# First weight blocks over the first rows, and attentions that open by their own counts

## Reference

```python
def even_layer(x, norm, w_in, ...):
    h = rmsnorm_2(x, norm)
    qa, ka, va, qb, kb, vb, gate = _split(h @ w_in, SPLIT_E)      # 3328 columns
    ...                                                            # two attentions
    o = jnp.concatenate([oa, ob], -1) * jax.nn.silu(gate)
    return o @ w_out
def odd_layer(x, norm, w_in, ...):
    h = rmsnorm_2(x, norm)
    cq, ckv, kpe, qd, kd, vd, gate = _split(h @ w_in, SPLIT_O)    # 2976 columns
    ...
```

## Time and profile before

| | us |
|---|---|
| median of 3 runs | 3122.36 |
| the runs | 3122.36, 3122.58, 3114.90 |
| the profiled execution | 3115.78 |
| its span | 3114.2 |
| TensorE busy | 2986.1 (96%) |
| VectorE, ScalarE, GpSimd busy | 1611.6, 1198.7, 1084.1 |

### The profile page before, as it was taken

One profiled execution on the slowest core, in us unless ns is written; L12 is line 12 of the kernel. 1 busy time (PEld: TensorE's weight loads), 2 busy tenths in 40 slices (PEclk: granted clock), 3 DMA queues, 4 the chain that ended last, 5 costly groups with the idle time before them and its releaser, 6 DMA issues.

```text
span 3114.2 us, 50002 instructions
## 1 busy us (share of the span) xinstructions
PE 2986.1 (96%) x18212; PEld 2593.1 (83%) x18212; DVE 1611.6 (52%) x3091; ACT 1198.7 (38%) x2181; POOL 1084.1 (35%) x702
## 2 busy tenths in 40 slices
PE   7999998999999999998999999999999999999989
PEld 6688866778888888888999888987897989988877
DVE  3899738342222232313038378971113958778861
ACT  3311264342221211313124356761323646667750
POOL 2222120432222235662226334335321554432235
PEclk9999998999999999999999999999999999999999
DMA  4123331431111114442296343405236763231223
GB/s 144 61 101 116 107 76 30 136 115 48 47 47 51 50 47 129 123 141 89 84 222 214 104 120 86 118 21 174 100 123 211 214 165 81 69 80 41 83 85 129
DMA packets 224247, 325.70 MB, mean 105 GB/s; under 512 B 81414, under 2 KB 167302, under 8 KB 221910
## 3 DMA queue, kind: packets, MB, share of 16 engines
q1 hardware_dynamic: 188934, 277.29, 29.8%
q10 hardware_dynamic: 33360, 39.98, 3.7%
q0 software_dynamic: 1792, 6.29, 0.7%
HBM read 229.95 MB, written 93.57 MB: 104 GB/s over the span
## 4 chain that ended last, share of the span: by engine, by line
PE 71%; DVE 8%; issue 2%; ACT 2%; POOL 1%; DMA 1%; SPq 0%; DVEq 0%; POOLq 0%; ACTq 0%
PE psum L2261 15%; PE psum L528 13%; PE psum L2047 8%; PE psum L2464 8%; PE psum L1097 6%; PE psum L1066 6%; PE psum L1077 5%; DVE arena L2865 3%; PE psum L780 2%; PE psum L758 2%; PE psum L769 1%; DVE arena L2854 1%; PE psum L1112 1%; PE psum L3224 1%; DVE above_mixer L840 1%
## 5 line engine op out<-in xcount | busy, mean ns | idle before, releaser
L2261 PE MATMUL psum<-parts_ffn 128*128 128x512 f32 x2112 | 482.2, 391 | 3.8 <-DVE parts_ffn L2218 3.8
L2261 PEld LDWEIGHTS psum<-parts_ffn 128*128 128x128 f32 x2112 | 398.4, 189 | 87.2 <-issue 2.2
L528 PE MATMUL psum<-parts_even,parts_ffn 128*128 128x256 f32 x2496 | 305.5, 285 | 5.2 <-DVE parts_ffn L2598 4.0
L528 PEld LDWEIGHTS psum<-parts_even,parts_ffn 128*128 128x128 f32 x2496 | 303.3, 194 | 5.9 <-DVE parts_ffn L2598 4.5
L2331 DVE SCALAR_TENSOR_TENSOR arena<-psum,arena 128x1023 f32<-128x1023 f32 x88 | 112.9, 1282 | 328.2 <-ACT arena L2315 322.0
L528 PE MATMUL psum<-parts_odd 128*128 128x248 f32 x2304 | 271.8, 280 | 4.9 <-ACT arena L568 2.2
L528 PEld LDWEIGHTS psum<-parts_odd 128*128 128x128 f32 x2304 | 269.7, 191 | 6.2 <-DVE parts_odd L2218 4.5
L568 ACT ACTIVATE arena<-psum 128x256 f32<-128x256 f32 (+2 forms) x240 | 87.8, 376 | 423.7 <-PE psum L528 419.7
L444 PE MATMUL psum<-parts_mixer 128*128 128x512 f32 x912 | 210.0, 391 | 0.3 <-DVE parts_mixer L287 0.3
L444 PEld LDWEIGHTS psum<-parts_mixer 128*128 128x128 f32 x912 | 170.5, 188 | 35.7 <-DVE parts_mixer L287 0.5
L1139 ACT ACTIVATE both<-psum 128x512 fp32r<-128x512 f32 x256 | 140.1, 596 | 107.6 <-PE psum L1077 107.0
(11 more groups left out here) (344 smaller groups left out, 5913.0 us busy)
## 6 DMA issues: line engine op xcount, KB each, us to landing
arena<-ffn_up_b SPq DMA_DIRECT2D x44, 512.0 KB, 3.3
arena<-ffn_down_k SPq DMA_DIRECT2D x44, 512.0 KB, 3.6
arena<-x SPq DMA_DIRECT2D x8, 2048.0 KB, 8.6
arena<-w_in_e SPq DMA_DIRECT2D x13, 1024.0 KB, 6.7
e_tokens<-arena ACTq DMA_DIRECT2D x26, 512.0 KB, 3.2
x<-arena SPq DMA_DIRECT2D x24, 512.0 KB, 3.8
arena<-w_in_o SPq DMA_DIRECT2D x12, 992.0 KB, 6.7
o_tokens<-arena ACTq DMA_DIRECT2D x24, 496.0 KB, 3.0
```

The source lines that it names most:

```text
L528: last = pe.matmul(self.bank(t), self.hT[:, a, k, t * P:(t + 1) * P], self.weights.parts[:, self.weights.slot(s), b, k, :], start=(k, a, b ...
L2261: last = pe.matmul(self.core.psum[:, 4 * u + 2 * s + h, :], parts[:, s, a, k, :], self.hT[:, b, k, h * HALF:(h + 1) * HALF], start=(k, a, ...
```

## The change

The first two blocks of `tok3a` and `tok4a` go in the order `FRONT`: (block 0, tiles 0 to 3), (block 1, tiles 0 to 3), (block 0, tiles 4 to 7), (block 1, tiles 4 to 7). The turns of half 1 stand behind positions 4 and 6 of this order instead of 1 and 3, and the hold for all parts behind position 7. ScalarE takes the first four positions out in the stage before: position 0 after `finish` of row tile 6, position 1 ahead of the parts of half 1, positions 2 and 3 behind its fourth part. In `tok4a` these four go to a stage of their own (`front_stage`) in the weight ring. `tok1`'s opening stands ahead of `feat1` on ScalarE, behind a hold for the scores. The first two of `expd` are added by TensorE itself, and `folded` is waited for at the first `back` step.

```diff
+    FRONT = [(s, 4 * h + j) for h in range(2) for s in range(2) for j in range(TT // 2)]
-    def multiply(self, pe, i, s, t):
+    def multiply(self, pe, i, s, t, at=None):
         if t == 0:
             self.weights.wait(pe, i, s)
-        pe.wait_ge(self.act_out, 16 * i + 8 * s + t + 1)
+        pe.wait_ge(self.act_out, (16 * i + 8 * s + t if at is None else at) + 1)
...
-        for s in range(2):
-            for t in range(TT):
-                if t == 4:
-                    hold(pe, self.second_half)
-                self.multiply(pe, 0, s, t)
-                if s == 0:
-                    self.between(pe, t)
+        for at, (s, t) in enumerate(self.FRONT):
+            if at == TT:
+                hold(pe, self.second_half)
+            self.multiply(pe, 0, s, t, at)
+            self.between(pe, at)
...
-    def take_out(self, act, i, s, t):
+    def take_front(self, act, at):
+        s, t = self.FRONT[at]
+        self.take_out(act, 0, s, t, at)
+    def take_out(self, act, i, s, t, front=None):
         h, j = divmod(t, TT // 2)
+        at, before = 16 * i + 8 * s + t, 2 * i + s
+        if front is not None:
+            at, h, before = front, front // 4 % 2, front // TT
+        stage = self.stage[:, h] if self.front_stage is None or front is None or front >= 4 else self.front_stage
         if j == 0:
-            act.wait_ge(self.stored[h], 16 * (2 * i + s) + 1)
+            act.wait_ge(self.stored[h], 16 * before + 1)
...
+        if self.between is not None:
+            for at in range(4, 2 * TT):
+                self.take_front(act, at)
+        for i, s in paired(act, self.blocks, 1 if self.between is not None else 0):
...
+        pe.sem_inc(self.expd, 2)
...
-        pe.wait_ge(self.folded, 1)
...
             g = n // 2
+            if g == 0:
+                pe.wait_ge(self.folded, 1)
...
-        act.sem_inc(self.expd, 2)
...
-        for k in range(KT) if t is None else {1: range(4), 3: range(4, KT)}.get(t, ()):
+        for k in range(KT) if t is None else {4: range(4), 6: range(4, KT)}.get(t, ()):
             self.turn(pe, 1, k)
...
             act.activation(self.ys[t], self.xs[:, t], ACT.Copy, scale=spot).then_inc(self.scaled, 1)
+            if t == 6 and self.take_next is not None:
+                self.take_next(act, 0)
...
         for k in range(KT):
+            if k in (0, 4) and self.take_next is not None:
+                for at in (1,) if k == 0 else (2, 3):
+                    self.take_next(act, at)
             part(act, 1, k)
...
+        tok1_opening = Part()
         add(scores)
...
+        add(tok1_opening)
         add(feat1)
...
+        def open_tok1(act):
+            hold(act, scores.done)
+            tok1.start_scalar(act)
+        tok1.opened_before = True
+        tok1_opening.methods = (None, None, open_tok1, None, None)
...
-                        [(0, 128, 13, e_heads)], [start_e + [first.done[n // 4]] for n in range(TT)], first_bank=4, stage_slots=1)
+                        [(0, 128, 13, e_heads)], [start_e + first.stored_blocks(2) + [first.done[n // 4]] for n in range(TT)], first_bank=4, stage_slots=1)
...
+        project.front_stage = shaped(core.arena[:, ring_at:ring_at + 4 * 248], (4, 248))
```

More of the change, by code:

```diff
@@ L492, in __init__ @@
         self.between, self.second_half, self.first_apart, self.opened_before = None, [], False, False
-        self.scalar_pieces, self.gates_from = {}, blocks * width
+        self.scalar_pieces, self.gates_from, self.front_stage = {}, blocks * width, None
         self.act_out = core.sem(f"{name}_act_out")
@@ L567, in take_out @@
             if a < b:
-                last = act.activation(self.stage[:, h, j, a:b], self.bank(t)[:, a:b], function)
+                last = act.activation(stage[:, j, a:b], self.bank(t)[:, a:b], function)
         last.then_inc(self.act_out, 1)
         if j == TT // 2 - 1:
-            act.wait_ge(self.act_out, 16 * i + 8 * s + t + 1 + len(self.banks))
+            act.wait_ge(self.act_out, at + 1 + len(self.banks))
             columns = self.out[t - j:t + 1, :, bass.ds((i * 2 + s) * self.width, self.width)]
-            act.dma_start(columns.rearrange("t p c -> p t c"), self.stage[:, h]).then_inc(self.stored[h], 16)
+            act.dma_start(columns.rearrange("t p c -> p t c"), stage).then_inc(self.stored[h], 16)
     def scalar(self, act):
@@ L579, in scalar @@
         if self.scalar_pieces:
-            for u in range(self.blocks * TT):
+            for at in range(4, 2 * TT):
+                self.take_front(act, at)
+            for u in range(2 * TT, self.blocks * TT):
                 b, t = divmod(u, TT)
@@ L585, in scalar @@
             return
-        for i, s in paired(act, self.blocks):
+        if self.between is not None:
+            for at in range(4, 2 * TT):
+                self.take_front(act, at)
+        for i, s in paired(act, self.blocks, 1 if self.between is not None else 0):
             for t in range(TT):
@@ L1960, in __init__ @@
         self.xs, self.ys, self.gain, self.after, self.retire = xs, ys, gain, after, retire
-        self.open_next, self.open_by_scalar, self.before_split = None, None, {}
+        self.open_next, self.open_by_scalar, self.before_split, self.take_next = None, None, {}, None
         self.K = w.shape[1]
@@ L2514, in turn_second @@
     def turn_second(self, pe, t):
-        for k in {1: range(4), 3: range(4, KT)}.get(t, ()):
+        for k in {4: range(4), 6: range(4, KT)}.get(t, ()):
             self.turn(pe, 1, k)
@@ L2563, in finish @@
             act.activation(self.y_of(t), self.x_of(t), ACT.Copy, scale=spot).then_inc(self.scaled, 1)
+            if t == 6:
+                self.take_next(act, 0)
         def part(act, h, k):
@@ L2572, in scalar @@
         self.order(act, self.high, drain, finish, part)
-        for k in range(KT):
+        self.take_next(act, 1)
+        for k in range(4):
+            part(act, 1, k)
+        for at in (2, 3):
+            self.take_next(act, at)
+        for k in range(4, KT):
             part(act, 1, k)
@@ L3575, in build @@
         project.first_apart = project.opened_before = True
-        down.open_next = project.start_scalar
+        down.open_next, down.take_next = project.start_scalar, project.take_front
         down.next_load = project.weights.load_first
@@ L3670, in build @@
         project.first_apart = project.opened_before = True
-        out3.open_by_scalar, out3.next_load = project.start_scalar, project.weights.load_first
+        out3.open_by_scalar, out3.next_load, out3.take_next = project.start_scalar, project.weights.load_first, project.take_front
+        project.front_stage = shaped(core.arena[:, ring_at:ring_at + 4 * 248], (4, 248))
         first = add(project)
```

## The result

The changed kernel takes 3095.53 us, median of four runs (3091.22 to 3098.26), against 3119.85 for the kernel before (3114.90 to 3122.58) measured with it: ratio 0.992, interval [0.991, 0.994], 24.3 us. Its profiled execution took 3098.26 (span 3096.6, mean granted clock 0.987), 17.5 less than the profiled one of before. Forecast: 3096. The two differences, 24.3 and 17.5, are a first hint that single traces carry draws of several us that are not the change's.

What follows compares the result with a forecast made beforehand. TensorE carries 71% of the chain that ended last. 6.2 + 11.0 + 4.0 + 2.1 = 23.3 us off the profiled 3115.78 gives 3092.5, off the runs' median 3122.36 gives 3099.1; forecast the middle, 3096, range 3084 to 3109.

Steps and rivals of the forecast that it cites:

- tok1, 6.2: tok1's start: early opening removes a 3.9 us stop and 2.6 of low clock; 6.2 us gained, bounds 3.9 and 6.7.
- Even boundary, 11.0: tok3a's start: stops of 5.09 and 2.23 us and the slow matmuls behind them go; 11.0 us gained, lower bound 7.3.
- the term of 1.7: Even boundary: the first tile behind the 2.23 us stop takes 2.97 instead of 4.67 us, 1.7 gained.
- Odd boundary, 4.0: tok4a's start: the 2.23 us stop before the second half and 1.8 of slow tile behind it go; 4.0 us gained.
- rival 1: Boundaries and tok1: stops go but the slow clock stays, 8.1 us less gain, 3104; chance 0.17.
- The covers: Even boundary: spare time of 3.1 us over the last row tile and 0.6 over the last parts, the thinnest.
- Attentions, 2.1: Attention starts: latent 1.0, axial 0.8, near 0.3, first and diff nothing; 2.1 us gained.
- rival 2: Latent: the half-clock stretch at 2766 may go too, up to 3 us more, 3093; chance 0.08.
- The choice of the middle, 3096: Whole kernel: runs lie at two levels 7 us apart, so the middle of 3092.5 and 3099.1; chance 0.60.
- (3): Behind the earlier projections (selection, loads at 385, head preparation): half the boundaries' gain lost, 3108; chance 0.08.
- (4): Both boundaries: the third block's split comes too late and stops TensorE, slower, 3126; chance 0.03.
- (5): Boundaries: takes in ScalarE's order hold the turns as long as before, no effect, 3117; chance 0.04.

Runs made afterwards that it cites:

- e1: The changed kernel again, unchanged; 3099.95 us median, ratio 0.992 to the kernel before.
- e2: The changed kernel with the five edits of the attentions undone; 3102.57 us, ratio 0.9934 to the kernel before.
- e5: The kernel before again, for a second trace of it; 3124.99 us, one run.
- e12: The changed kernel with the bias's load and spread ahead of tok3b's first weight loads, VectorE's clearing ahead of the gains' scaling; 3091.28 us, ratio 0.992.
- e7: The changed kernel with the second half's turns one position later, at 5 and 7; 3109.91 us, ratio 0.9963 to the kernel before.
- e4: The changed kernel with both boundaries in the old order; 3112.00 us, ratio 0.9969 to the kernel before.
- e10: The kernel before with the bias's load and spread moved earlier, VectorE's clearing behind the gains' scaling; 3169.47 us, ratio 1.0154.
- e3: The changed kernel with tok1's opening back at its old place; 3104.52 us, ratio 0.9941 to the kernel before.
- e9: The changed kernel with the bias's load and spread moved earlier, VectorE's clearing behind the gains' scaling; 3145.68 us, ratio 1.0084 to the kernel before.
- e8: The changed kernel with tok3b and tok4b opened by TensorE itself, tok3b bank by bank; 3097.13 us, ratio 0.9923 to the kernel before.
- e11: The changed kernel with the earlier bias spread (clearing behind the scaling) and tok3b and tok4b opened by TensorE; 3146.91 us, ratio 1.0081.
- e6: The changed kernel with its new row order but the second half's turns back at positions 1 and 3; 3105.55 us, ratio 0.9951.

## Why the prediction was right, point by point

**tok1, 6.2.** Right. The place gives 6.8 in all ten traces with the edit and 0.5 on the mean of four without: 6.3. The stop is 3.86 in each; the low clock behind it is the part that varies: against the changed kernel's 12.5 us, the 105 matmuls from tok1's start take 15.2, 14.9, 14.9 and 14.1. I took the first of these, the longest. My own sign against it, a mixer loop that starts less than 5 us earlier, came true (3.4 earlier), and misled: the trace after had lost 1.4 us at start-up, before any edit, and 1.9 more behind the gate rows' load (stop 5.82 against 3.90), which draws in every trace. A sign stated as an absolute time must be taken from a lead at the edit's own place.

**Even boundary, 11.0.** Right: eight traces with the new order give 9.4 to 11.3, mean 10.6, four with the old one 0.0. Its spread is something that the sum had not seen. tok3a's first 47 matmuls, behind a stop of 1.6 to 1.8 us, take 7.0 us in nine of the fourteen traces and 8.3 in five. In four of these five the clock was low before the start already (0.50 at 1413.50 to 1416.00 in the trace after, where the same turns in e1 had 1.00), and the stop ahead of tok3a is 1.57 instead of 1.79; e2 is slow without that sign, and e10 quick with it. In the old order a slow start costs almost nothing, as the stop for the normalized row tile ends at a time that ScalarE sets: in e5 the start is slow and that stop is 3.2 us instead of 5.1. The new order took away this buffer, so it gives 11.3 behind a quick start and 9.4 to 10.0 behind a slow one (after, e2, e12). The terms were right for the quick start: from the 48th matmul on, all eight traces give 11.3 against the trace before. The first tile behind the 2.23 takes 4.3 to 4.5 us in all four traces of the old order, so here the term of 1.7 held, though e7 shows the same stop without it.

**Odd boundary, 4.0.** Right in kind, 0.8 too much: 4.6 on the mean of the same eight, and 1.4 of four in the old order, 3.2. The term that was mis-sized is the 1.8 of low clock behind the stop. I read it off one trace. All four traces of the old order have the stop of 2.23, but the tile behind it takes 4.37 us, from its start to the next one's, in the trace before alone, and 2.86 to 2.89 in e4, e5 and e10 (clock 0.50 and 1.00, rows under e4): a draw, as rival 1 had it. From the 48th matmul of tok4a on, the new order gives 4.0 against the trace before and 2.6 against the mean of the other three. The trace before also has the slowest start of tok4a of all (8.24 us for 47 matmuls, 7.1 to 8.16 in the others), and with both it lies 1.9 under the other three old ones. The covers held: 0.6 us over the last parts was enough, and e7 shows what it costs if it goes.

**Attentions, 2.1.** Under-sized: axial 1.1 for 0.8, near 0.1 for 0.3, latent 1.5 for 1.0, sum 2.7, or 3.4 with the draws behind 2790 (e2). The mechanism of the stop was right, and nothing was gained at the first attention, as I had it. The term that was mis-sized is the low clock behind latent's stop, which I had put at nothing in the sum and only rival 2 had.

**Sum.** 6.3 + 10.6 + 3.2 + 2.7 = 22.8 by the places (23.5 with latent's later draws), 23.3 forecast, 24.3 and 23.8 by the times (after, and the means of e1). By experiments that undo one part each, the ratios of e2, e3 and e4 less that of e1 give 0.0014 + 0.0021 + 0.0049 = 0.0084 (26 us), where the whole change is 0.0080.

**The choice of the middle, 3096.** Right by luck as much as by reason. I saw two levels of the runs 7 us apart and could not name them. Now two of the draws are named: the head preparation (0 to -8 us) and the gate rows' load and what follows (0.9 to -5.8 between 369 and 1400). Each is as large as the distance between the levels.

**Rivals.** (1), the low clock stays: fell at tok1 and the even boundary, which give 6.3 and 10.6 where the stops alone are 3.9 and 7.3. At the odd boundary its price of 1.8 was a draw to begin with, and its second ground, that slow stretches come and go by chance, is shown there, at latent and at tok3a's start. The Trainium skill's page "TensorE: Matmul & The Clock Gate" (section "Part 1: The HAM clock gate") tells of a cold count that varies from run to run; the 7.0 and 8.3 of one and the same start agree with it. (2), latent gains its clock: the stretch at 2766 is quick in all ten traces with the edit, the trace after too, but also in two of four without it, so some 0.6 us go with the edit instead of up to 3; the later stretches hide it in three of the ten. (3), given back later: nothing shows it, and a small one is not excluded. My 3108 for it was a slip: half of the boundaries' 15.0 from 3096 gives 3103.5. What looked like a give-back at the head preparation (13.6 to 12.1 in the trace after) is a draw that the kernel before has too (0 and -5.9 in its two traces, -5.7 on the mean of eight with some or all of the edits), and with the store out of the way nothing is given back (e9 against e10). At diff's start four of the ten traces with the new row order lose 2.0 to 5.6 and none of the four without; two of the four are e8 and e11, with an edit more. (4) fell: the third block's splits are in time at both boundaries; no stop for line 404 appears in a trace of the changed kernel. (5) fell with e4.

**What stays open.** Why diff's start stops TensorE 5.4 us in e8 and 2.2 in the trace after: both kernels with tok3b's and tok4b's own openings (e8, e11) have the long one, two others (e3, e6) one of 3.8 and 3.9. Whether the new row order has a part in it, since all four have it. And whether moving the spread pays in time.

## What to carry to other kernels

An engine that stops for the last row tile of a stage wants work between that does not need it: a second weight block over the first half's rows gave 14 us at two boundaries, and the place of the turns in it matters as much (three tiles earlier cost 6 us at one boundary, one tile later 10 at two). Before a gain under 1% is read from two traces, take a second trace of each kernel and compare them place by place, by the count of matmuls: here one place moved by 5 to 6 us between two executions of the same kernel (0 and -5.9 before the change, -1.5 and -6.9 after it). A slow stretch behind a stop needs the same care: one trace priced it at 1.8 us where three others of the same row order had none. A stop that ends at another engine's time is also a buffer for slow matmuls ahead of it, which is lost with the stop.

## What the runs showed of the hardware

One and the same stop of TensorE is followed by either level of its clock. Behind 1.33 to 1.42 us in latent it was low in seven of fourteen traces (0.56 against 1.00 in the two stretches under e2). Behind 2.23 us at the odd boundary it was low (0.50) in one of four traces, and behind 2.23 at the even boundary in four of four; with the turns one position later (e7) it was the other way round. Behind a stop of 3.9 us at tok1 the slow time was 1.6 to 2.7 us in four traces.

A single store of 3810 KB in pieces of 508 bytes took 38 to 40 us and kept the DMA engines busy all that time; 13 us of it moved 140 GB/s in all. A weight load issued while it ran held SyncE's queue for 13 to 18 us (28 to 29 in e9 to e11, where it stands right behind the store), and a load of the head preparation issued as it ended took 5.3 to 10.8 us to its first use (5.3 and 8.8 in two traces of the kernel before, 6.9 to 10.8 in eight others); with the store moved ahead (e12) these were 0.33 and 5.2.
